# FFN down projection as seven block products in three rounds, in a one-core transformer step

## The reference

```python
D_MODEL = 1024; FFN_HIDDEN = 2816

def swiglu(h, w1, w3, w2):
    return (jax.nn.silu(h @ w1) * (h @ w3)) @ w2

# x = x + gate2 * swiglu(modulate(x, norm2_g, shift2, scale2), ffn_w1, ffn_w3, ffn_w2)
```

## Time and profile before

| what | value |
|---|---|
| median of 3 runs | 1391.97 us (1389.74 to 1392.6) |
| the profiled execution | 1391.43 us |
| its span | 1389.6 us |
| TensorE busy in the span | 98% |
| VectorE, ScalarE, GpSimd busy | 58%, 48%, 16% |

### The profile page before, as it was taken

The page is one execution under the profiler, slowest core; times in us unless marked ns, Lnnn a source line. Parts: engine busy times, 40 slices in busy tenths (PEclk is TensorE's granted clock), DMA queues, the critical chain, the costliest instruction groups (busy, mean ns, idle before and its releaser), DMA issues.

```text
span 1389.6 us, 26249 instructions
## 1 busy us (share of the span) xinstructions
...
## 2 busy tenths in 40 slices
...
GB/s 309 203 134 90 154 96 112 87 84 99 85 109 96 113 86 91 102 46 114 120 82 220 69 69 137 152 76 62 62 91 62 104 93 62 92 92 62 84 92 69
DMA packets 202560, 144.49 MB, mean 104 GB/s; under 512 B 8719, under 2 KB 188215, under 8 KB 202183
## 3 DMA queue, kind: packets, MB, share of 16 engines
q1 hardware_dynamic: 202439, 142.82, 34.7%
...
...
## 4 chain that ended last, share of the span: by engine, by line
PE 89%; DMA 2%; DVE 2%; SPq 2%; ACT 2%; issue 1%; DVEq 0%; ACTq 0%
PE ps L1195 30%; PE ps L1733 17%; PE ps L1770 11%; PE ps L1497 8%; PE ps L1720 2%; PE ps L1432 2%; PE ps L1367 2%; PE ps L1629 2%; PE ps L1341 1%; PE ps L1439 1%; PE ps L1373 1%; PE ps L1174 1%; PE ps L1597 1%; PE ps L1269 1%; PE ps L1699 1%
## 5 line engine op out<-in xcount | busy, mean ns | idle before, releaser
L1195 PE MATMUL ps<-hT_r,WAH_r 128*128 128x320 f32 x912 | 228.2, 331 | 4.0 <-DVE naT_r L2610 1.3
L1195 PE MATMUL ps<-xT_r,WAH_r 128*128 128x320 f32 x912 | 207.5, 309 | 0.0
L1195 PEld LDWEIGHTS ps<-hT_r,WAH_r 128*128 128x128 f32 x912 | 145.1, 189 | 20.2 <-issue 11.6
L1195 PEld LDWEIGHTS ps<-xT_r,WAH_r 128*128 128x128 f32 x912 | 152.7, 188 | 0.0
L1195 PE MATMUL ps<-hT_r,W_r 128*128 128x320 f32 x592 | 133.8, 309 | 0.0
L1770 PE MATMUL ps<-a_part,W_r 128*128 128x320 f32 x704 | 132.3, 310 | 0.0
L3167 POOL TENSOR_TENSOR gm<-sqkq,dt 128x1280 f32<-128x1280 f32 x8 | 23.5, 2934 | 566.2 <-DVE Xc L2652 496.2
L1770 PEld LDWEIGHTS ps<-a_part,W_r 128*128 128x128 f32 x704 | 110.3, 188 | 0.0
L1733 PE MATMUL ps<-t_big_r,W_r 128*128 128x320 f32 x380 | 107.2, 310 | 0.5 <-ACT naT L2317 0.4
L1733 PE MATMUL ps<-b_part,W_r 128*128 128x320 f32 x456 | 101.3, 309 | 0.0
L1195 PEld LDWEIGHTS ps<-hT_r,W_r 128*128 128x128 f32 x592 | 99.1, 189 | 0.0
...
## 6 DMA issues: line engine op xcount, KB each, us to landing
...
```

Source lines behind the costliest of these rows:

```text
L1195: m = e.matmul(ps[:, bank + b, 0:n], w[:, k, :], x[:, k, a:a + n], start=k == 0 and i == 0, stop=k == KD - 1 and i == 2, skip_group_check= ...
```

## The change

The down projection gets the same seven-product form as the up projection. The hidden tiles come in three rounds of 8, 8 and 6. A list TURNS holds 22 "up" turns (numbered 0 to 7, 12 to 19, 24 to 29) and after each round four "down" turns (8 to 11, 20 to 23, 30 to 33), one for each pair of output tiles g. A down turn uses the weight slots, banks and product order of an up turn. Its blocks are output tile s by even or odd hidden tiles: 4 k-tiles per product in rounds one and two, 3 in the last. 84, 84 and 63 matmuls are in a down turn. The other operand is made of pairs of hidden tiles: B11, B21, B22 are halves of the even or the odd tile, and D1 to D4 are differences of them (`sum_down`), each 128x320, each rounded by ScalarE (`hid_big`) and split by VectorE (`hid_small`). VectorE adds each product to x straight from its bank, in seven steps (`result`), and TensorE waits for four of them inside the turn.

```diff
+ROUNDS = (range(0, 8), range(8, 16), range(16, KF))
+AT_LAST = {3: ("B11 0", "D1 0"), 4: ("D2 1", "D3 1", "B22 1"), 5: ("B21 1", "D4 1")}
+AT_FIRST = {3: ("sum D1 0", "sum D2 1", "sum D3 1", "sum D4 1"), 4: ("B11 0", "D1 0"), 5: ("D2 1", "D3 1", "B22 1"), 6: ("B21 1", "D4 1")}
...
-            def down(q, g, s):
-                wait(dve_ff, f"down {q} {g} {s}")
...
-                        for b, (a, c) in enumerate(HALVES):
-                            m = e.matmul(ps[:, DOWN_BANKS[s] + b, 0:c], w, a_part[xp][:, tile_of(k), a:a + c], start=k == 0 and n == 0, stop=k == KH - 1 and n == 2, skip_group_check=True)
+            def down(n):
+
+                q, g = TURNS[n][1]
+                a, f, x = 6 + n % 2, 2, 3
+                read_by(n - 2, "hid", "y21")
+                product(n, "A11", a, True)
+                if q == len(ROUNDS) - 1 and g:
+                    for s in range(2):
+                        turn_y(g - 1, s)
+                read_by(n - 1, "C12", "y12b")
+                product(n, "S1", x, True)
+                wait(dve_ff, f"y11a {n}")
+                product(n, "S2", a, False)
+                read_by(n - 1, "C11", "y11b")
+                product(n, "A12", f, True)
+                wait(dve_ff, f"y12a {n}")
+                product(n, "S3", a, False)
+                wait(dve_ff, f"y22b {n}")
+                product(n, "S4", x, False)
+                wait(dve_ff, f"y22a {n}")
+                product(n, "A22", a, False)
```

ScalarE in an up turn:

```diff
-                    keep("snap1", p)
-                    if inner:
-                        plain_big(p + 1, "A11")
-                    keep("s5", p)
+                    keep("snap1", n)
+                    for d in ("B21", "D4") if even(n) and n - 1 in UPS else ("B11", "D1") if not even(n) else ():
+                        hid_big(n - 1, d)
+                    plain_big(n + 1, "A11")
+                    keep("s5", n)
+                    keep("snap2", n)
...
+                    else:
+                        joint = TURNS[n + 1][0] == "down"
+                        hid_big(n, "D2")
+                        sum_big(n + 1, "S3")
+                        if joint:
+                            hid_big(n, "B21")
+                        hid_big(n, "D3")
+                        hid_big(n, "B22")
+                        sum_big(n + 1, "S4")
+                        plain_big(n + 1, "A22")
```

VectorE, the differences and the results:

```diff
+            def sum_down(n, d):
+
+                x, less, made = {"D1": ("B22", "B11", f"hid {n}"), "D2": ("B22", "D1", f"hid1 {n}"), "D3": ("B22", None, f"hid1 {n}"), "D4": ("B21", "D2", f"hid {n}")}[d]
...
+            def result(n, step):
+
+                q, g = TURNS[n][1]
+                product, bank = {"y11a": ("P1", 6 + n % 2), "y22b": ("P5", 3), "y12a": ("P6", 6 + n % 2), "y11b": ("P2", 2), "y22a": ("P7", 6 + n % 2), "y12b": ("P3", 3), "y21": ("P4", 6 + n % 2)}[step]
...
+                for a, w, c in ((HT, LAT - HT, 0), (LAT, CTX, 1)) if half else ((0, HT, 0),):
+                    x = xT[:, 2 * g + s, a:a + w]
+                    m = e.scalar_tensor_tensor(x, ps[:, bank, a - half * HT:a - half * HT + w], mods[:, 2 * g + s + 40, c:c + 1], x, ALU.mult, ALU.add)
```

More of the change, by code:

```diff
@@ L274, in pe_ff_steps, with tiles_half, place_of, even @@
+def tiles_half(n):
+    return len(ROUNDS[round_of(n)]) // 2 if TURNS[n][0] == "down" else KD // 2
+def place_of(n):
+    return TURNS[n][1] - ROUNDS[round_of(n)].start
+def even(n):
+    return place_of(n) % 2 == 0
+def last_up(n):
+    return max(u for u in UPS if u < n)
+def last_of_kind(n, odd):
+    return max(u for u in UPS if u < n and even(u) != odd)
 def pe_ff_steps():
     names = ["up 0"]
[L276 to L302, removed]
-def act_ff_steps():
[L306 to L315, removed]
-                names += [f"snap2 {p}", w[1], f"silu0 {p}", w[2], w[3], f"silu1 {p}", *w[4:], f"hid {p}"]
-            else:
-                names += [f"snap1 {p}", f"s5 {p}", f"snap2 {p}", f"silu0 {p}", w[0], f"silu1 {p}", w[1], f"hid {p}"]
[L319 to L323, removed]
-    return names + [f"y {GD - 1} 1"]
```

596 lines of the change are left out of this document (329 added, 267 removed).

## The result

The changed kernel takes 1396.62 us (median of 5 runs, 1395.71 to 1398.41) beside 1392.45 us of the kernel before (5 runs, 1389.74 to 1393.48). The ratio is 1.004, with a 95% interval of 1.0028 to 1.0052: slower by 0.4%, where the prediction had said faster by 0.2%. It lies above the predicted range.

The account below looks back on a forecast made before the run. From 993.96 us on TensorE was taken to bound the kernel nearly throughout. Saving 20.7 us less stalls of 17.9 left 2.8 us gained, from 1391.43 to 1388.6 us; range 1378 to 1395.

Parts of the forecast that it names:

- The saving of 20.7 us: Gain side: 132 fewer down matmuls (19.4 us), plus the round's start in the middle, fewer roundings and a shorter end.
- snap2 of tile 3: Tile 3: ScalarE's copy snap2 comes late behind the rounding of D1, so P7 waits 2.9 us.
- Turns 9 and 21 wait for y11a: Second down turn of rounds one and two: P6 waits 1.6 us, or 2.8 if another sum gets in; 2.2 taken.
- the rival of a backlog that doesn't clear: Turns 10, 11, 22, 23: y11a stays late as in 9 and 21, 2.2 us each, 1397 us; chance 15%.
- The last round: Last down turns, with shorter products: waits for D2, y12a, y22a and y21, at most 3.0 us, 2.6 taken.
- Result pieces, with one matrix in PSUM, don't wait for GpSimd: VectorE's result pieces: 1.13 us beside a GpSimd sum of 1.30; the forecast sum left out up to 4.4 us a down turn.
- the clock: After a long TensorE wait the clock may fall, costing 0 to 1.7 us, kept inside the range; no separate chance given.
- the restarts: After any TensorE wait that ends late: 0.07 to 0.2 us more than the lateness itself.
- The first two down turns: Start of the down turns in rounds one and two: VectorE's queue delays products by 2.5 us, twice, 5.0 us.
- even tiles after an odd one, later rounds: Turns 14, 16, 18, 26, 28: snap1 ends at 3.7, P6 due at 3.53; 0.3 us each, 1.5 us together.
- the early tiles: Tiles 3 to 6: stalls of 3.7 us in tile 3 and 5.1 us in tiles 4 to 6.
- on average there is room: VectorE in a down turn: 8.0 us of work in 12.34 us, so cost arises only where an order gives no room.

Follow-up runs that it names:

- the run with fills: Changed kernel with GpSimd's four sums of weight blocks replaced, from turn 4 on, by writing a constant (products wrong): 1375.4 us, ratio 0.9892.

## Why the prediction was wrong

**Right.** The saving of 20.7 us is borne out by the run with fills, to the 1.5 us that stay open. The 132 matmuls are gone, and one takes 0.147 us still. snap2 of tile 3 is late for the reason given, VectorE's step ahead of it held up by a sum, 2.98 us for 2.9: in the changed kernel's timeline ScalarE waits 4.61 us for D1's difference, and snap2 stands behind it.

```profile
1000.77 0.47 ACT L2370 ACTIVATE d_part_r<-d_sum 128x320 fp32r<-128x320 f32 x1 [4.61 <-DVE d_sum L3072]
1001.15 0.61 ACT L2301 ACTIVATE W_r<-oT 128x512 fp32r<-128x512 f32 x1
1001.67 0.42 ACT L2356 ACTIVATE c<-ps 128x320 f32<-128x320 f32 x1
1001.98 0.43 ACT L2356 ACTIVATE naT<-ps 128x320 f32<-128x320 f32 x1
```

Turns 9 and 21 wait for y11a (1.65 and 1.46, predicted 1.6 to 2.8 and taken as 2.2), turns 10, 11, 22 and 23 don't: the rival of a backlog that doesn't clear gave nearly the measured time, 1397, but not by what happened. So its closeness to 1397 is luck. The last round came to 2.2 for 2.6. Result pieces, with one matrix in PSUM, don't wait for GpSimd, as said: beside its sums the pieces of 320 columns take 0.54 us as ever.

**Wrong, the terms that were mis-sized.** The forecast had 17.9 us of cost against 20.7 saved; the traces have 25.1, and so 2.8 us to be gained became 4.4 lost. The step that failed is that only one awaited step was followed through the later even turns, and that the clock and the restarts had no term of their own: 5.4 us for 1.5, 3.4 for none and 2.0 for tenths added here and there. The first two down turns gave back 1.9 (3.1 for 5.0). First, "even tiles after an odd one, later rounds": 0.3 each, bounds 0 and 5, measured 1.07 each, 5.4 together. Only snap1 was followed there. C22, worked out for the early tiles as standing "behind S1 and another sum", was not followed in the later ones, where the same third sum meets the same small part of S1: P4 waits 0.78. Second, the early tiles: 8.8 predicted, 8.9 measured, the total right by luck, since 0.8 for C22 in tile 3 and 0.9 in tile 5 weren't there while C22 in tiles 4 and 6 cost 2.51 each instead of 1.1, and snap1 there 0.30 and 0.63 instead of 1.0. Third, the clock stood in the range with at most 1.7 us and outside the sum. After the waits in turns 3 and 4 the granted clock is 0.68 for 5.4 us, between the two levels (1.2 and 2.4 GHz) and so some time on the lower one; after the wait of turn 6, as long as that of turn 4, it is not:

```profile
1002.40:1007.80 5.40, 5.34 (x26) 5.34 (x27) 4.71 (x11) 2.77 (x7) 1.75 (x1) 0.68 0.60 163
...
1022.80:1028.20 5.40, 5.35 (x26) 5.35 (x27) 4.51 (x9) 2.87 (x7) 0.00 (x0) 0.68 0.00 0
1052.40:1057.80 5.40, 5.40 (x37) 5.40 (x38) 4.71 (x9) 3.64 (x8) 0.00 (x0) 1.00 0.01 3
```

5.4 x 0.32 is 1.7 us each, 3.4 together. The chain says the same from the other side, behind the wait of turn 3, where 24 matmuls take 5.33 us and 3.53 were due (24 x 0.147):

```profile
1002.46 5.33 PE ps L1769 x24
```

Fourth, the restart, priced at 0.07 to 0.2 us, went into single stalls as a rounding up; twenty at 0.1 are 2 us.

**Why it leaned one way.** Each term had been worked out as the lateness of one step against a free TensorE, with "on average there is room" on VectorE. There is room for work, and none for 1.1 us that comes when P7 ends. The rule from the Trainium skill that the prediction drew on (SBUF — State Buffer, section Who interferes with whom) held here in every run: VectorE's instructions with both inputs in SBUF take up to 1.6 to 1.8 us instead of 0.5 to 0.7 beside GpSimd's sums, not beside its fills, and result pieces aren't touched. What was missing was to ask of each awaited step what is released at the same moment as it. C22 and the third sum are both released by the end of P7; so in turns 14, 16, 18, 26 and 28 the sum met the small part of S1 that stood ahead of C22.

**What stays open.** In the run of the changed kernel with fills and in the one with four sums on VectorE, gaps and restarts sum to some 1.5 us less than the part's length asks for. Whether a wait of 2.2 to 2.7 us lowers the clock was not settled: of eight such waits in the profiles, four did. In turns 3 and 4 TensorE waits 5.8 us in the changed kernel and 3.4 with the sums on VectorE; no order of mine removed the 3.4, and that it is the differences and small parts of tiles 0 and 1 is argued from the order: no run took them away.
